# Moving a convolution's channel sums, norm and last step one slot sooner in a hand-ordered two-layer kernel

## The chip, the cores and the metric

The kernel runs on one core of one Trainium2 chip. The core has a matrix engine (TensorE, called PE in the profile), a vector engine (DVE), an activation engine (ACT), a small general engine (POOL) and a queue engine that issues transfers (SP). The metric is the device time of one execution in microseconds (us). Lower is better.

## The reference, cut to what matters

`x` is 256 positions by 2048 channels in float32. A first block (attention branches) gives `x`, and a second block follows. The change lies in the mixing layer of the second block:

```python
y = _rms(h, norm_mix_g)
z = y @ w_in                                   # 2048 -> 4608 columns
za, zb, zc, zd = jnp.split(z, split_at, axis=-1)
oa = _mixer_sgu(za, ...)                       # gated unit
ob = _mixer_shortconv(zb, sc_conv_w)           # 3 taps
oc = _mixer_conformer(zc, cf_conv_w, ...)      # 31 taps, then layer norm, then silu
od = _mixer_pool(zd, pool_w, pool_scale)       # windowed means, then a product
h = h + jnp.concatenate([oa, ob, oc, od], axis=-1) @ w_out

def _mixer_conformer(z, conv_w, conv_b, ln_g, ln_b):
    a, g = jnp.split(z, 2, axis=-1)
    h = a * jax.nn.sigmoid(g)
    h = _causal_dwconv(h, conv_w) + conv_b
    h = _ln(h, ln_g, ln_b)                     # mean and variance over 512 channels
    return jax.nn.silu(h)
```

A feed-forward layer, a gated product with `p` and a last norm follow.

## The kernel before

All large products stream float32 weights from memory. Each weight tile is a "unit": SP loads it into `raw` (5 buffers), ACT copies it into `hi` (4 buffers, rounded to the matrix engine's fast format), DVE writes the rest `raw - hi` into `lo` (in the place of `raw`), and PE makes three products per block, hi x hi, hi x lo and lo x hi (the helper `three`, lines 477 to 479). There are 370 units in one fixed order (`plan`). Groups of four units make one output tile of 512 columns, in one of two halves of PSUM tile `psA`.

Each engine runs its own program, and the order in each is written by hand. For every unit number u, PE runs `side(u)` (small extra products into `psB`) and then `unit(u)`. ACT and DVE run `side(u)`, then `split(u + 3)` (the hi copy on ACT, line 855; the lo subtraction on DVE, line 1244), and after the last unit of a group `post(group)`. For u in `EARLY`, ACT makes its split ahead of its side work. ACT's `split(u + 3)` waits until PE has finished unit u - 1, and DVE's waits for ACT's. So every step is a slot of its engine's queue: a wait in it holds back all that stands behind it. Nothing else ties the slots of the engines together, and DVE may run a slot behind PE.

The units around the change, all of the mixing layer of the second block: 170 to 177 (the convolution's inputs), 178 to 181 `v2`, 182 to 185 `u2`, 186 to 189 `zd`, 190 to 193 `scc`, 194 to 197 `sch`, 198 to 201 `bg`, and 202 to 217 `out2`, the product with `w_out`. Units 178 to 181 and 202 to 217 are of kind N, those of the other names of kind T: 4 blocks x 4 column groups x 3 = 48 matmuls of 256 columns. The four units of one `out2` group take the mixers' parts in `MIX_ORDER` and wait for the semaphore `mix_low` 1, 2, 3, 4.

The side work that matters:

- The 31-tap convolution runs on DVE, channel block by channel block, on `CA`: 124 instructions of line 1443 and 1445 (`conv_tap`), spread over the slots 177 to 194, most with seven. Each adds one to `conv_taps`. The last four stand at the head of DVE's slot 194.
- `channel_sum(psB[:, 0, 0:256], CA, ...)` (line 749) is PE's: four products with a matrix of ones that add up the 512 channels. It waits for `conv_taps` 124, before `unit(u)` of its slot.
- ACT copies the mean to `ST` (line 1045, semaphore `cm_made`). DVE subtracts it (line 1581, `ca_centered`). ACT squares (line 1047, `cv_squared`). PE adds up the squares (line 749 again, `var_dotted`). DVE makes the inverse root (lines 1585 and 1212 to 1217) and scales (line 1587, `ca_normed`). ACT applies gain and bias and makes a tanh (lines 1056, 1058, `cn_tanh`). DVE finishes the silu (line 1607, `cn_made`). ACT and DVE write the hi and lo parts for `out2` (lines 951 and 1460).
- The pooling mixer: `pool_sums` and `pool_means` on DVE (lines 1465 to 1480, semaphore `pool_ready`), its product on PE (line 799, `pool_dotted`), then ACT's and DVE's hi and lo parts (lines 1051 and 1611).
- The short convolution: lines 1590 to 1604 on DVE.
- A helper `finish` makes DVE or ACT wait for the instruction just issued.

Of the kernel before, what the change touches and what calls it, by code (L numbers as in the profile page):

```python
# [10 lines left out]
ACT = mybir.ActivationFunctionType  # L11
# [48 lines left out]

K16 = [[(4 * q + k, 4 * q + k) for k in range(4)] for q in range(4)]
K8 = [[(8 * q + k, 8 * q + k) for k in range(8)] for q in range(2)]
MIX_ORDER = (0, 3, 2, 1)


def plan(A):
# [60 lines left out]
def build_hybrid(nc, A, C, out, scratch):  # L127
    with ExitStack() as ctx:
# [98 lines left out]
        P2 = B[:, 1:3, :].rearrange("p a b -> p (a b)")[:, 0:1088].rearrange("p (c n) -> p c n", c=4)  # L227
        PA = B4[:, :].rearrange("p (c n) -> p c n", c=4)
        SCt = B4[:, 0:1040].rearrange("p (c n) -> p c n", c=4)
        SQ = PW[:, 0:2, :].rearrange("p g d -> p (g d)")  # L230

        psA = ctx.enter_context(nc.psum_tensor("psA", [128, 2, 1024], F32))
        psB = ctx.enter_context(nc.psum_tensor("psB", [128, 2, 1024], F32))
# [106 lines left out]
        TOPK = {21 + n: (2 * n, 2 * n + 1) for n in range(4)}  # L340
        FORGET = {27 + h: h for h in range(4)}
        ATTEND = {s + i: (b, i) for b, s, n in ((0, 32, 6), (1, 43, 6), (2, 59, 11), (3, 75, 6)) for i in range(n)}
        EARLY = (196, 199, 200)
        ATTENDED = {38: 0, 49: 1, 72: 2, 81: 3}
        MERGE = {95 + 20 * f: f for f in range(4)}
        TURN1 = {160 + 4 * f: f for f in range(4)}
# [128 lines left out]
        def tensor_program(e):  # L475
# [276 lines left out]
            def side(u):  # L752
                if u == 1:
                    turn_x(1)
                if u == 6:
                    vectors()
                    e.wait_ge(rd_made, 1)
                    e.wait_ge(xl_made, 3)
                    e.matmul(psB[:, 0, 0:256], ONE, RD[:, :], start=True, stop=True).then_inc(rx_spread, 1)
                if u == 7:  # L760
                    biases()
                if u == 12:
                    spread()
                if u in HEADS:
                    index_heads(HEADS[u][0] // 4)
                if u == 26:
                    forget_sums()
                if u in FORGET:
                    forget_head(FORGET[u])
                if u in ATTEND:  # L770
                    attend(*ATTEND[u])
                if u in ATTENDED:
                    attended(ATTENDED[u])
                if u in MERGE:
                    merge(MERGE[u])
                if u in TURN1:
                    e.wait_ge(h_made, TURN1[u] + 1)
                    turn_h(FIRST + TURN1[u], TURN1[u])
                if u == 172:
                    e.wait_ge(srd_made, 1)  # L780
                    e.wait_ge(ss2_made, 4)
                    e.matmul(psB[:, 0, 0:256], ONE, ST[:, 0, :], start=True, stop=True).then_inc(sb_dotted, 1)
                if u == 175:
                    e.wait_ge(sw_landed, 16)
                    e.wait_ge(sb_made, 1)
                    for h in range(4):
                        x = e.transpose(psB[:, 0, 128 * h:128 * h + 128], B[:, 1, 128 * h:128 * h + 128], ID[:, :])
                    x.then_inc(sw_turned, 1)
                if u == 196:
                    e.wait_ge(conv_taps, 124)  # L790
                    e.wait_ge(sw_made, 1)
                    channel_sum(psB[:, 0, 0:256], CA, cm_dotted)
                if u == 198:
                    ps, w4 = c4(psB[:, 1, :]), c4(B[:, 3, :])
                    e.wait_ge(pool_ready, 1)
                    e.wait_ge(pw_landed, 16)
                    e.wait_ge(sgu_made, 1)
                    for g in range(4):
                        x = e.matmul(ps[:, g, :], PW[:, g, :], w4[:, g, :], start=True, stop=True)
                    x.then_inc(pool_dotted, 1)  # L800
                if u == 198:
                    e.wait_ge(cv_squared, 1)
                    channel_sum(psB[:, 0, 512:768], CB, var_dotted)
                if u in TURN2:
                    e.wait_ge(bank_dve, freed(("out2", TURN2[u])))
                    turn_h(SECOND + TURN2[u], TURN2[u])
                if u == 221:
                    ps = psB[:, 0, 0:512].rearrange("p (k t) -> p k t", k=2)
                    e.wait_ge(p_landed, 16)
                    e.wait_ge(ss3_made, 4)  # L810
                    for k in range(2):
                        for t in range(2):
                            x = e.transpose(ps[:, k, 128 * t:128 * t + 128], PP[:, t, 128 * k:128 * k + 128], ID[:, :])
                    x.then_inc(p_turned, 1)
                if u in TURNH:
                    j = TURNH[u]
                    e.wait_ge(bank_dve, freed(("fu", j)))
                    e.wait_ge(flip_low, HIDDEN + j)
                    flip(lambda t, k: HB[:, t, 128 * k:128 * k + 128], 1)
                if u in TURN3:  # L820
                    e.wait_ge(bank_dve, freed(("down", 8 + TURN3[u])))
                    turn_h(THIRD + TURN3[u], TURN3[u])
# [17 lines left out]
        def scalar_program(e):  # L840
# [112 lines left out]
            def side(u):  # L953
# [86 lines left out]
                if u == 194:  # L1040
                    e.wait_ge(sgu_made, 1)
                    part_high(c4(B[:, 3, :]), 0, 0.5)
                if u == 196:
                    e.wait_ge(cm_dotted, 1)
                    e.activation(ST[:, 0, :], psB[:, 0, 0:256], ACT.Copy, scale=1.0 / 512).then_inc(cm_made, 1)
                    e.wait_ge(ca_centered, 1)
                    e.activation(CB[:, :, :], CA[:, :, :], ACT.Square).then_inc(cv_squared, 1)
                if u == 198:
                    e.wait_ge(pool_dotted, 1)
                    for g in range(4):  # L1050
                        x = e.activation(YH[:, 12 + g, :], c4(psB[:, 1, :])[:, g, :], ACT.Copy, scale=VC[:, 76 + g:77 + g])
                    x.then_inc(mix_high, 1)
                if u == 199:
                    e.wait_ge(ca_normed, 1)
                    for c in range(4):
                        x = e.activation(CA[:, c, :], CA[:, c, :], ACT.Identity, scale=VC[:, 68 + c:69 + c], bias=VC[:, 72 + c:73 + c])
                    finish(x)
                    e.activation(CB[:, :, :], CA[:, :, :], ACT.Tanh, scale=0.5).then_inc(cn_tanh, 1)
                if u == 200:
                    e.wait_ge(cn_made, 1)  # L1060
                    part_high(CA[:, :, :], 2, 0.5)
                if u in TURN2:
                    f = TURN2[u]
                    high(SECOND + f, XH[:, 4 * f:4 * f + 4, :], 1, scale_cols(32, f))
# [136 lines left out]
        def vector_program(e):  # L1201
# [281 lines left out]
            def side(u):  # L1483
# [89 lines left out]
                    gelu_poly(B[:, 3, :], B[:, 2, :], 2)  # L1573
                if u == 194:
                    part_low(c4(B[:, 3, :]), 0, 0.5, 1)
                    pool_sums()
                if u == 195:
                    pool_means()
                if u == 196:
                    e.wait_ge(cm_made, 1)  # L1580
                    e.tensor_tensor(CA[:, :, :], CA[:, :, :], over(ST[:, 0, :], 4), ALU.subtract).then_inc(ca_centered, 1)
                if u == 198:
                    v_, y_, w_ = ST[:, 0, :], ST[:, 1, :], ST[:, 2, :]
                    e.wait_ge(var_dotted, 1)
                    finish(e.tensor_scalar(v_, psB[:, 0, 512:768], 1.0 / 512, EPS, ALU.mult, ALU.add))
                    rsqrt(v_, y_, w_)
                    e.tensor_tensor(CA[:, :, :], CA[:, :, :], over(y_, 4), ALU.mult).then_inc(ca_normed, 1)
                    y = c4(B[:, 2, :])
                    e.wait_ge(sb_made, 1)
                    finish(e.tensor_tensor(SQ, SB[:, :], SB[:, :], ALU.mult))  # L1590
# [2 lines left out]
                    for c in range(4):  # L1593
                        e.tensor_scalar(y[:, c, :], SCt[:, c, 0:256], VC[:, 81 + c:82 + c], None, ALU.mult).then_inc(short_taps, 1)
                if u == 199:
                    y = c4(B[:, 2, :])
                    for j in (1, 2):
                        for c in range(4):
                            e.wait_ge(short_taps, 4 * j - 3 + c)
                            e.scalar_tensor_tensor(out=y[:, c, :], in0=SCt[:, c, j:j + 256],  # L1600
                                                   scalar=VC[:, 81 + 4 * j + c:82 + 4 * j + c], in1=y[:, c, :],
                                                   op0=ALU.mult, op1=ALU.add).then_inc(short_taps, 1)
                    e.wait_ge(short_taps, 12)
                    finish(e.tensor_tensor(y, y, over(SB[:, :], 4), ALU.mult))
                if u == 200:
                    e.wait_ge(cn_tanh, 1)
                    e.scalar_tensor_tensor(out=CA[:, :, :], in0=CB[:, :, :], scalar=1.0, in1=CA[:, :, :], op0=ALU.add,
                                           op1=ALU.mult).then_inc(cn_made, 1)
                    e.wait_ge(mix_high, 2)
                    for g in range(4):  # L1610
                        x = e.scalar_tensor_tensor(out=YL[:, 12 + g, :], in0=c4(psB[:, 1, :])[:, g, :], scalar=VC[:, 76 + g:77 + g],
                                                   in1=YH[:, 12 + g, :].bitcast(F32), op0=ALU.mult, op1=ALU.subtract)
                    x.then_inc(mix_low, 1)
                    part_low(CA[:, :, :], 2, 0.5, 3)
                if u in TURN2:
                    f = TURN2[u]
                    low(SECOND + f, XL[:, 4 * f:4 * f + 4, :], XH[:, 4 * f:4 * f + 4, :], 1, scale_cols(32, f))
# [240 lines left out]
```

## Time and profile before

| | |
|---|---|
| median of 3 runs | 2116.52 us (2116.45 to 2117.03) |
| the profiled execution's own time | 2116.6 us |
| its span in the trace | 2114.8 us |
| PE busy | 2101.7 us, 99% |
| PE weight loads busy (beside the matmuls) | 1788.5 us, 85% |
| DVE busy | 1215.1 us, 57% |
| ACT busy | 901.8 us, 43% |
| bytes moved | 398.34 MB, mean 188 GB/s |

The span is the time from the first to the last instruction of the profiled execution; the time of the execution has 1.8 us more around it. An engine's busy time counts its own instructions, not its waits. A matmul's shown duration overlaps the next one's, since they are pipelined, so the step from start to start is what one costs. For an fp32 product that isn't in the fast format the trace keeps two records for one matmul instruction, so a channel sum of four matmuls has eight. The granted clock is the share of full speed at which TensorE's clock ran.

### The profile page before, as it was taken

What the parts mean: (1) busy time and instruction counts of PE and PEld (TensorE: products, weight loads), DVE (VectorE), ACT (ScalarE), POOL (GpSimd) and SP (SyncE); (2) the same over time, 40 slices, a digit from 0 to 9 for tenths busy, and PEclk for the clock granted to TensorE, in tenths of its full rate; (3) what the DMA queues carried; (4) which work ended last, traced back from release to release, by engine and by line L of the source; (5) the groups of instructions that cost most, each with busy time, mean ns of one, the idle gap of its engine ahead of it and who ended that gap; (6) DMA issues with size and microseconds to landing.
All of it is one profiled execution on the core that took longest, in us unless ns stands there. A gap on an engine that the chain in (4) does not pass through costs nothing.

```text
span 2114.8 us, 24862 instructions
## 1 busy us (share of the span) xinstructions
PE 2101.7 (99%) x10607; PEld 1788.5 (85%) x10607; DVE 1215.1 (57%) x1211; ACT 901.8 (43%) x858; POOL 21.1 (1%) x40
## 2 busy tenths in 40 slices
PE   9999999999999999999999999999999999999998
PEld 8888888888888888888999888888888888888887
DVE  5576555665545544456889855545445454454555
ACT  5444443544443443445354444343333433334443
POOL 2000000000000000000000000000000000000000
PEclk9999999999999999999999999999999999999999
DMA  8655555555655555575655556555555555565553
GB/s 245 212 178 178 166 171 182 171 175 173 199 182 196 192 188 197 192 246 180 206 187 171 179 179 195 189 187 191 198 188 191 184 194 196 187 195 182 195 201 120
DMA packets 224685, 398.34 MB, mean 188 GB/s; under 512 B 11154, under 2 KB 56458, under 8 KB 224320
## 3 DMA queue, kind: packets, MB, share of 16 engines
q1 hardware_dynamic: 221296, 387.64, 56.0%
q0 software_dynamic: 2528, 8.00, 1.3%
q8 instruction: 84, 1.38, 0.3%
q10 hardware_dynamic: 752, 1.12, 0.1%
q14 instruction: 25, 0.20, 0.0%
HBM read 394.62 MB, written 2.12 MB: 188 GB/s over the span
## 4 chain that ended last, share of the span: by engine, by line
PE 95%; DVE 4%; ACT 1%; issue 0%; ACTq 0%
PE psA L477 27%; PE psA L479 27%; PE psA L478 27%; PE psA L530 6%; PE psA L534 3%; DVE CA L1445 1%; PE psB L589 1%; DVE lo L1244 1%; PE psB L689 0%; PE psB L715 0%; PE psA L826 0%; PE psB L637 0%; PE psB L749 0%; ACT hi L855 0%; PE psB L676 0%
## 5 line engine op out<-in xcount | busy, mean ns | idle before, releaser
L1244 DVE TENSOR_TENSOR lo<-raw,hi 128x2048 fp32r<-128x2048 f32 x369 | 837.1, 2272 | 618.2 <-ACT hi L855 616.0
L855 ACT ACTIVATE hi<-raw 128x2048 fp32r<-128x2048 f32 x369 | 699.6, 1900 | 685.4 <-PE psA L479 583.2
L477 PE MATMUL psA<-hi,XHL 128*128 128x512 f32 x1632 | 637.9, 391 | 0.0
L479 PE MATMUL psA<-hi,XHL 128*128 128x512 f32 x1632 | 633.9, 388 | 0.0
L478 PE MATMUL psA<-lo,XHL 128*128 128x512 f32 x1632 | 633.4, 388 | 0.0
L479 PEld LDWEIGHTS psA<-hi,XHL 128*128 128x128 f32 x1632 | 306.3, 188 | 63.6
L477 PEld LDWEIGHTS psA<-hi,XHL 128*128 128x128 f32 x1632 | 306.5, 188 | 62.6 <-issue 0.4
L478 PEld LDWEIGHTS psA<-lo,XHL 128*128 128x128 f32 x1632 | 306.6, 188 | 61.7
L477 PE MATMUL psA<-hi,YH 128*128 128x512 f32 x608 | 237.2, 390 | 0.0
L479 PE MATMUL psA<-hi,YL 128*128 128x512 f32 x608 | 236.6, 389 | 0.0
L478 PE MATMUL psA<-lo,YH 128*128 128x512 f32 x608 | 236.6, 389 | 0.0
L477 PE MATMUL psA<-XHL,hi 128*128 128x256 f32 (+1 forms) x528 | 150.2, 284 | 1.2 <-DVE lo L1284 1.2
L478 PE MATMUL psA<-XHL,hi 128*128 128x256 f32 (+1 forms) x528 | 149.3, 283 | 0.0
L479 PE MATMUL psA<-XHL,lo 128*128 128x256 f32 (+1 forms) x528 | 149.3, 283 | 0.0
L530 PE MATMUL psA<-XHL,hi 128*128 128x512 f32 x576 | 138.6, 393 | 0.0
L479 PEld LDWEIGHTS psA<-hi,YL 128*128 128x128 f32 x608 | 114.1, 188 | 23.7
L477 PEld LDWEIGHTS psA<-hi,YH 128*128 128x128 f32 x608 | 114.1, 188 | 23.5
L478 PEld LDWEIGHTS psA<-lo,YH 128*128 128x128 f32 x608 | 114.2, 188 | 23.4
L530 PEld LDWEIGHTS psA<-XHL,hi 128*128 128x128 f32 x576 | 105.9, 188 | 21.5 <-issue 0.6
L477 PEld LDWEIGHTS psA<-XHL,hi 128*128 128x128 f32 (+1 forms) x528 | 100.7, 191 | 1.7 <-DVE XHL L1291 1.6
L478 PEld LDWEIGHTS psA<-XHL,hi 128*128 128x128 f32 (+1 forms) x528 | 100.7, 191 | 0.2
L479 PEld LDWEIGHTS psA<-XHL,lo 128*128 128x128 f32 (+1 forms) x528 | 100.7, 191 | 0.0
(355 smaller groups left out, 1273.6 us busy)
## 6 DMA issues: line engine op xcount, KB each, us to landing
raw<-in_w_in_dram SPq DMA_DIRECT2D x159, 1024.0 KB, 5.1
raw<-in_w_gate_dram SPq DMA_DIRECT2D x44, 1024.0 KB, 5.2
raw<-in_w_up_dram SPq DMA_DIRECT2D x44, 1024.0 KB, 5.2
raw<-in_w_down_dram SPq DMA_DIRECT2D x44, 1024.0 KB, 5.1
raw<-in_w_out_dram SPq DMA_DIRECT2D x32, 1024.0 KB, 5.1
raw<-in_w_branch_dram SPq DMA_DIRECT2D x16, 1024.0 KB, 5.0
raw<-in_w_ple_gate_dram SPq DMA_DIRECT2D x16, 1024.0 KB, 5.0
raw<-in_w_in_dram SPq DMA_DIRECT2D x16, 512.0 KB, 4.7
```

Of the source, the lines that this page charges most:

```text
L477: e.matmul(dst, A2[0], B2[0], start=first, stop=False, skip_group_check=True)
L478: e.matmul(dst, A2[0], B2[1], start=False, stop=False, skip_group_check=True)
L479: return e.matmul(dst, A2[1], B2[0], start=False, stop=last, skip_group_check=True)
L530: e.matmul(both, hh[:, s], XHL[:, kb, :, :].rearrange("p a t -> p (a t)"), start=i == 0 and n < 2, stop=False, skip_group_check=True)
L534: x = e.matmul(both[:, 256:512], ll[:, s], XH[:, kb, :], start=False, stop=i == len(g.parts) - 1 and n >= 14, skip_group_check=True)
L589: x = e.transpose(ps[:, k, 128 * t:128 * t + 128], src(t, k), ID[:, :])
L855: e.activation(hi[u % H][:, 0:m], raw[u % R][:, 0:m], ACT.Copy).then_inc(hi_made, 1)
L1244: e.tensor_tensor(lo[u % R][:, 0:m], raw[u % R][:, 0:m], hi[u % H][:, 0:m].bitcast(F32), ALU.subtract).then_inc(lo_made, 1)
L1445: x = e.scalar_tensor_tensor(out=CA[:, c, :], in0=HP[:, c, j:j + 256], scalar=CW[:, 4 * j + c:4 * j + c + 1], in1=CA[:, c, :], op0=ALU.mul ...
```

## The change

The convolution's steps after its taps are moved to earlier slots, and the pooling mixer's steps behind them. The parts of `out2` are taken in the order 0, 2, 3, 1 (gated unit, convolution, pooling, short convolution) in place of 0, 3, 2, 1. ACT's `EARLY` slots become 195, 198 and 199. A scratch tile `SQ` lies in `SW` and no more in `PW`, since the pooling product reads `PW` later than before relative to it.

| step | engine | slot before | slot after |
|---|---|---|---|
| channel sum of `CA` | PE | 196 | 195 |
| mean, square | ACT | 196 | 195 |
| subtract the mean | DVE | 196 | 195, behind `pool_sums` |
| `pool_sums` / `pool_means` | DVE | 194 / 195 | 195 / 196 |
| channel sum of the squares | PE | 198 | 197 |
| inverse root and scaling | DVE | 198 | 197 |
| short convolution, start | DVE | 198 | 198 |
| gain, bias, tanh | ACT | 199 | 198 |
| end of the silu, its hi and lo parts | DVE, ACT | 200 | 199 |
| pooling product | PE | 198 | 198 |
| its hi part | ACT | 198 | 199, behind the convolution's |
| its lo part | DVE | 200, ahead of the convolution's | 200 |

```diff
-MIX_ORDER = (0, 3, 2, 1)
+MIX_ORDER = (0, 2, 3, 1)
...
-        SQ = PW[:, 0:2, :].rearrange("p g d -> p (g d)")
+        SQ = SW[:, 0:2, :].rearrange("p g d -> p (g d)")
...
-        EARLY = (196, 199, 200)
+        EARLY = (195, 198, 199)
...
# tensor_program, side(u)
-                if u == 196:
+                if u == 195:
                     e.wait_ge(conv_taps, 124)
                     e.wait_ge(sw_made, 1)
                     channel_sum(psB[:, 0, 0:256], CA, cm_dotted)
...
-                if u == 198:
+                if u == 197:
                     e.wait_ge(cv_squared, 1)
                     channel_sum(psB[:, 0, 512:768], CB, var_dotted)
...
# scalar_program, side(u)
-                if u == 196:
+                if u == 195:
                     e.wait_ge(cm_dotted, 1)
                     e.activation(ST[:, 0, :], psB[:, 0, 0:256], ACT.Copy, scale=1.0 / 512).then_inc(cm_made, 1)
                     e.wait_ge(ca_centered, 1)
                     e.activation(CB[:, :, :], CA[:, :, :], ACT.Square).then_inc(cv_squared, 1)
                 if u == 198:
-                    e.wait_ge(pool_dotted, 1)
-                    for g in range(4):
-                        x = e.activation(YH[:, 12 + g, :], c4(psB[:, 1, :])[:, g, :], ACT.Copy, scale=VC[:, 76 + g:77 + g])
-                    x.then_inc(mix_high, 1)
-                if u == 199:
                     e.wait_ge(ca_normed, 1)
...
-                if u == 200:
+                if u == 199:
                     e.wait_ge(cn_made, 1)
                     part_high(CA[:, :, :], 2, 0.5)
+                    e.wait_ge(pool_dotted, 1)
+                    for g in range(4):
+                        x = e.activation(YH[:, 12 + g, :], c4(psB[:, 1, :])[:, g, :], ACT.Copy, scale=VC[:, 76 + g:77 + g])
+                    x.then_inc(mix_high, 1)
...
# vector_program, side(u)
                 if u == 194:
                     part_low(c4(B[:, 3, :]), 0, 0.5, 1)
+                if u == 195:
                     pool_sums()
-                if u == 195:
-                    pool_means()
-                if u == 196:
                     e.wait_ge(cm_made, 1)
                     e.tensor_tensor(CA[:, :, :], CA[:, :, :], over(ST[:, 0, :], 4), ALU.subtract).then_inc(ca_centered, 1)
-                if u == 198:
+                if u == 196:
+                    pool_means()
+                if u == 197:
                     v_, y_, w_ = ST[:, 0, :], ST[:, 1, :], ST[:, 2, :]
                     e.wait_ge(var_dotted, 1)
...
+                if u == 198:
                     y = c4(B[:, 2, :])
...
                 if u == 199:
+                    e.wait_ge(cn_tanh, 1)
+                    e.scalar_tensor_tensor(out=CA[:, :, :], in0=CB[:, :, :], scalar=1.0, in1=CA[:, :, :], op0=ALU.add,
+                                           op1=ALU.mult).then_inc(cn_made, 1)
                     y = c4(B[:, 2, :])
...
+                    part_low(CA[:, :, :], 2, 0.5, 2)
                     e.wait_ge(short_taps, 12)
                     finish(e.tensor_tensor(y, y, over(SB[:, :], 4), ALU.mult))
                 if u == 200:
-                    e.wait_ge(cn_tanh, 1)
-                    e.scalar_tensor_tensor(out=CA[:, :, :], in0=CB[:, :, :], scalar=1.0, in1=CA[:, :, :], op0=ALU.add,
-                                           op1=ALU.mult).then_inc(cn_made, 1)
-                    e.wait_ge(mix_high, 2)
+                    e.wait_ge(mix_high, 3)
...
-                    part_low(CA[:, :, :], 2, 0.5, 3)
```

## Rows read from the trace of the kernel before

**Rows 1.** The page: busy time by engine, and the chain that ended last.

```profile
PE 2101.7 (99%) x10607; PEld 1788.5 (85%) x10607; DVE 1215.1 (57%) x1211; ACT 901.8 (43%) x858; POOL 21.1 (1%) x40
...
PE 95%; DVE 4%; ACT 1%; issue 0%; ACTq 0%
```

**Rows 2.** All waits of PE: us in total, times, longest.

```profile
PE psA L826 <- DVE QI L1751: 2.0, 1, 2.0
PE psA L477 <- DVE lo L1284: 1.2, 1, 1.2
PE psB L749 <- DVE CA L1445: 0.3, 1, 0.3
```

**Rows 3.** Timeline of PE, 1129 to 1146: start, us, instructions, idle before.

```profile
1129.99 1.95 PE L744 MATMUL psB<-SW,B 128*128 128x128 f32 x16
1131.69 0.36 PE L477 MATMUL psA<-XHL,hi 128*128 128x256 f32 x1
...
1137.41 0.28 PE L479 MATMUL psA<-XHL,lo 128*128 128x256 f32 x1
1137.53 0.28 PE L477 MATMUL psA<-XHL,hi 128*128 128x256 f32 x1
...
1143.17 0.28 PE L479 MATMUL psA<-XHL,lo 128*128 128x256 f32 x1
1143.70 1.99 PE L749 MATMUL psB<-CA,TR 128*128 128x256 f32 x8 [0.25 <-DVE CA L1445]
1145.35 0.47 PE L477 MATMUL psA<-XHL,hi 128*128 128x256 f32 x1
```

**Rows 4.** All waits of DVE from 1100 to 1200.

```profile
DVE lo L1244 <- ACT hi L855: 1.3, 2, 0.7
DVE YL L1460 <- ACT YH L951: 1.1, 1, 1.1
```

**Rows 5.** Timeline of DVE, 1136 to 1185.

```profile
1136.06 2.29 DVE L1244 TENSOR_TENSOR lo<-raw,hi 128x2048 fp32r<-128x2048 f32 x1
...
1141.98 1.67 DVE L1445 SCALAR_TENSOR_TENSOR CA<-HP,CW,CA 128x256 f32<-128x256 f32 x4
1143.56 1.22 DVE L1460 SCALAR_TENSOR_TENSOR YL<-B,YH 128x1024 fp32r<-128x1024 f32 x1
1144.75 0.11 DVE L1465 MEMSET B<- 128x64 f32 x1
...
1147.04 2.29 DVE L1244 TENSOR_TENSOR lo<-raw,hi 128x2048 fp32r<-128x2048 f32 x1
1149.25 0.68 DVE L1473 TENSOR_TENSOR B<-B 128x512 f32<-128x512 f32 x1
...
1152.62 2.29 DVE L1244 TENSOR_TENSOR lo<-raw,hi 128x2048 fp32r<-128x2048 f32 x1
1154.82 1.22 DVE L1581 TENSOR_TENSOR CA<-CA,ST 128x1024 f32<-128x1024 f32 x1
...
1162.32 0.41 DVE L1585 TENSOR_SCALAR ST<-psB 128x256 f32<-128x256 f32 x1
...
1167.57 1.23 DVE L1587 TENSOR_TENSOR CA<-CA,ST 128x1024 f32<-128x1024 f32 x1
1168.71 0.42 DVE L1590 TENSOR_TENSOR PW<-SB 128x256 f32<-128x256 f32 x1
...
1183.15 1.22 DVE L1460 SCALAR_TENSOR_TENSOR YL<-CA,YH 128x1024 fp32r<-128x1024 f32 x1
```

**Rows 6.** Timeline of ACT, 1142 to 1149.

```profile
1143.07 5.50 ACT L855 ACTIVATE hi<-raw 128x2048 fp32r<-128x2048 f32 x3
1148.47 0.36 ACT L1045 ACTIVATE ST<-psB 128x256 f32<-128x256 f32 x1
```

**Rows 7.** Timeline of PE where the execution begins.

```profile
2.02 4.64 PE L826 MATMUL psA<-QI 128*128 128x256 f32 x10 [2.02 <-DVE QI L1751]
6.59 0.28 PE L828 MATMUL psB<-ID,VN 16*128 16x16 f32 x1
```

**Rows 8.** Windows at the end: us, PE, PEld, DVE, ACT, POOL, granted clock, DMA.

```profile
2105.00:2106.00 1.00, 0.20 (x2) 0.00 (x0) 0.20 (x1) 0.77 (x3) 0.00 (x0) 1.00 1.02 379
...
2109.00:2109.50 0.50, 0.00 (x0) 0.00 (x0) 0.43 (x3) 0.14 (x1) 0.00 (x0) 0.96 0.00 0
2109.50:2110.00 0.50, 0.00 (x0) 0.00 (x0) 0.50 (x1) 0.50 (x2) 0.00 (x0) 0.50 0.00 0
```

## The prediction

> **What bounds the kernel.** I read the page first: PE is busy for 99% of the span and makes up 95% of the chain that ended last [rows 1]. Then I asked for every wait of PE. There are three, 3.5 us together, and two of them (2.0 and 1.2 us) lie where the execution begins. The third is the channel sum of line 749, which waits 0.3 us for a convolution tap of line 1445 [rows 2]. So behind the first few us PE has no idle time that this change could take away, except these 0.3 us. And whatever wait the change adds to PE goes to the end in full, since no later idle time of PE is there to absorb it.
>
> The third view is the timeline around that one wait. On PE the product of line 744, which stands behind unit 193, begins at 1129.99. Unit 194 begins at 1131.69. It has 48 matmuls, 0.12 us from start to start (1137.41 to 1137.53), so 5.76 us, which puts the beginning of unit 195 near 1137.5, and its last matmul starts at 1143.17. The channel sum of slot 196 then begins at 1143.70, 0.25 us after PE ran dry, and unit 196 follows at 1145.35 [rows 3]. On DVE the last four taps begin at 1141.98 and take 1.67 us, so they end at about 1143.65 [rows 5]. The tap's end, PE's idle 0.25 us and the start of the channel sum fit one another. The reader is to see that in slot 196 PE meets the taps almost exactly as they end.
>
> **Part 1, the channel sum one slot sooner: where the time goes.** In the changed kernel PE comes to this wait before unit 195, at about 1137.5. The question is when the 124th tap ends there. On DVE no instruction ahead of the last tap is moved: the change of DVE's slots starts behind the lo part of line 1460, which follows the taps. From 1100 to 1200 DVE waited three times only, for 2.4 us in all [rows 4], and none of these waits lies between 1136 and 1144, where one instruction follows the other; the taps are late since DVE is full, not since it waits for PE. ACT's moved steps also stand behind slot 194. So the last tap still ends at about 1143.65, and the channel sum still begins at 1143.70. PE idles from about 1137.65 (the last matmul of unit 194 started at 1137.41 and takes 0.28 us) to 1143.70: 6.0 us in place of 0.25.
>
> What PE loses is one unit: before, unit 195 was done in these 5.76 us, and now it comes behind the channel sum. After the channel sum before stood unit 196 at 1145.35; now unit 195 stands there and unit 196 begins 5.76 us later, at 1151.1. From both sides: if the taps ended 0.25 us sooner for some reason, the loss would be 5.5; if PE needs as long to take up work again as the first matmul of unit 196 shows (0.47 for 0.28 us), 5.95. I take 5.8 us.
>
> **Part 2, the clock behind a stall.** The trace of before has no PE stall of this length in mid-course, so its effect on the clock is bounded by the two ends of the execution. At the end, PE's last matmul lies in the first 0.20 us of the window from 2105, and the granted clock is at 1.00 until the window from 2109.0 to 2109.5, where its mean is 0.96, and then 0.50 [rows 8]: it fell to the lower level (1.2 GHz) some 4.3 us after the last matmul. The stall that I expect is 6.0 us. At the beginning, ten records of 256 columns take from 2.02 to 6.59 [rows 7], 0.46 us each, where eight records of the same shape in the channel sum took 1143.70 to 1145.35, 0.206 each [rows 3]. (The profile's clock column shows 1.00 there; the durations are those of the lower level.) So PE ran for about 4.6 us at the lower level before it came to 2.4 GHz.
>
> Put behind the stall, this would cost: eight records of the channel sum at 0.46 instead of 0.206 us, 3.7 us for 1.65, a loss of 2.0; and the 0.9 us left of 4.6 in unit 195's matmuls, where half speed loses about half, 0.45. Together 2.5 us. Lower bound 0 (the clock holds), upper bound 3.5 (the lower level lasts 2 us longer than at the beginning). I take 2.5, since 6.0 us of idleness is longer than the 4.3 us after which the clock fell at the end.
>
> The Trainium skill ("TensorE: Matmul & The Clock Gate", "HAM oscillation — how this bites in real kernels") says that a pause of the matrix engine in mid-kernel can drop its clock to half, and that it must work for some time before it gets full speed back. By that rule the sum has Part 2 in it and comes to 2124.8; without it, it would be 2122.3. The fall in [rows 8] agrees with the rule; no row here shows one between two stretches of work.
>
> **Part 3, the rest of the moved chain: costs nothing, and gains nothing.** Nothing of it is new work: the instructions and their shapes are the same, no transfer is issued by any of them, and SP and POOL aren't touched. What can cost is a later `split` behind a new wait. I follow the slots with the durations of the rows, from a channel sum that ends at 1145.4 (with the clock's 2 us, 1147.4; PE's own times shift as much or more).
> - DVE slot 194 ends with the lo split, which can begin once ACT's copy, begun at 1143.07 [rows 6], is there at 1145.0: done 1147.2. `pool_sums` takes from 1144.75 to 1147.04 in [rows 5], so 2.3: 1149.5. ACT has by then made its early split and the mean (0.36 us [rows 6]). The mean is subtracted by 1150.7, ACT's square of about 1.1 us is there by 1151.8, and PE wants it before unit 197, at 1156.9: 5 us spare. Behind DVE's wait for the mean stands its split for unit 198, done at 1152.9; PE wants it at about 1166.
> - `pool_means` (1149.25 to 1152.62, 3.4 us [rows 5]) ends at 1156.3, the split for unit 199 at 1158.5. PE wants `pool_ready` before unit 198, at about 1164.5: 8 us spare.
> - Slot 197: the sum of the squares is there at 1158.6. From line 1585 to the end of line 1587 took 1162.32 to 1168.8, 6.5 us [rows 5]: 1165.2, and behind it the split for unit 200, done at 1167.4. PE wants that at about 1177.6: 10 us spare.
> - Slots 198 to 200 hold the same DVE work as before in another order (1168.71 to 1184.4 with splits in it [rows 5]). It ends at about 1184, and the third unit of `out2` wants the pooling part at about 1200. PE has 6 us to spare at the tightest, the split for unit 202.
>
> So the convolution's part is ready a few us sooner relative to PE, but its reader never waited: [rows 2] have no wait for `mix_low`. If this slack weren't there, each late split would cost PE its lateness; the smallest slack is 5 us.
>
> **The sum.** Against the profiled execution's own time of 2116.6 us (span 2114.8): + 5.8 + 2.5 = 2124.9. The runs' median is 0.1 us lower, so the time for the runs is 2124.8 us.
>
> **The rivals.**
> - The clock holds through the stall. Then only the unit's time is lost: 2116.5 + 5.8 = 2122.3. For it: the granted clock at the end held for 4.3 us, so the stall outlasts it by less than 2 us, and where the fall comes may vary. Against it: 6.0 is still the longer time.
> - Another stall behind the first one: DVE's slots 195 to 197 now put lo splits behind waits for ACT and PE. It would show as line 477 waiting for line 1244. It decides if a link of the chain slips by over the 5 us of slack. Price: what it slips beyond that, some 2 us, so about 2127. Against it: every slack above is twice an instruction's length or more.
> - On the other side, faster or no change: DVE reaches its last tap sooner, before PE runs dry. For this the work of 1136.06 to 1141.98 on DVE (a split, line 1456, the `scc` step) would have to be gone from before the taps. It decides from a last tap that ends by about 1137.7, 6 us sooner; then even the 0.25 us of idle time go, and the time is 2116.3. I see nothing in the diff that moves any of it, and the wait is for all 124 taps, not for the first channel block's.
> - The change doesn't do what it says: the compiled order would be the written one, as the queues are in order, so I give it nothing of its own; it is in the case before.
>
> **Chances.** Stall and clock, 2124.8: 0.62. Clock holds, 2122.3: 0.23. A further stall, 2127: 0.07. No added stall of weight: 0.08, of which 0.02 for faster. The range holds the first two: from 2121.8 (5.5 for the unit, less 0.2 for the runs' spread) to 2126.0 (5.95 and 3.5). The likeliest case alone spans 2123.5 to 2126.0. A measurement of this kernel tells about 0.2% (4.2 us) from no change, so slower begins at 2120.7: the first three cases are all beyond it. Slower 0.92, same 0.06, faster 0.02.
>
> **What would show each step.** Right: PE's waits have line 749 on line 1445 with about 6 us in place of 0.3; the last taps still begin near 1142.0 and the channel sum at 1143.7; the windows around 1141 to 1148 show a granted clock below 1.00, and the eight records of the channel sum take about 3.7 us; no other wait of PE is longer than before. Wrong: the channel sum starts sooner than 1143, or PE waits for a lo split later, or the channel sum after the stall takes 1.65 us, which would be the clock that holds.

## The result, and the profile after

The changed kernel takes 2124.64 us in the median of 6 runs (2124.14 to 2125.13), the kernel before 2116.78 (2116.4 to 2117.28, 6 runs on the same chip). The ratio is 1.0037 (95% interval 1.0027 to 1.0048), so the change makes the kernel slower by 7.9 us. The profiled execution took 2125.03 us, with a span of 2123.2 against 2114.8 before.

All waits of PE in the changed kernel, to be read against [rows 2] (columns: us in total, times, longest):

```profile
PE psB L749 <- DVE CA L1444: 6.0, 1, 6.0
PE psA L826 <- DVE QI L1751: 2.0, 1, 2.0
PE psA L477 <- DVE lo L1283: 1.2, 1, 1.2
```

The two waits at the beginning are as before. The channel sum's wait for the last tap (line 1444 here, 1445 before) has grown from 0.3 to 6.0 us, and no wait for a lo split or for `mix_low` has come up. PE's timeline there, to be read against [rows 3]:

```profile
1137.18 0.28 PE L479 MATMUL psA<-XHL,lo 128*128 128x256 f32 x1
1143.46 3.78 PE L749 MATMUL psB<-CA,TR 128*128 128x256 f32 x8 [6.00 <-DVE CA L1444]
1146.68 0.78 PE L477 MATMUL psA<-XHL,hi 128*128 128x256 f32 x1
1147.25 0.41 PE L478 MATMUL psA<-XHL,hi 128*128 128x256 f32 x1
1147.47 0.41 PE L479 MATMUL psA<-XHL,lo 128*128 128x256 f32 x1
...
1149.60 0.30 PE L477 MATMUL psA<-XHL,hi 128*128 128x256 f32 x1
1149.74 0.28 PE L478 MATMUL psA<-XHL,hi 128*128 128x256 f32 x1
1149.86 0.28 PE L479 MATMUL psA<-XHL,lo 128*128 128x256 f32 x1
...
1191.94 0.40 PE L477 MATMUL psA<-hi,YH 128*128 128x512 f32 x1
```

The channel sum starts at 1143.46, where it started at 1143.70 before; this execution began its weight stream 0.23 us sooner. The unit that follows is 195, not 196. The eight records of the sum now reach from 1143.46 to 1146.68, 3.2 us in place of 1.65, and the unit's first matmuls are 0.21 us apart, where from 1149.74 they are 0.12 us apart as everywhere else. The windows around the pause show why (columns: window, its length, PE, PEld, DVE, ACT and POOL busy with counts, granted clock, DMA share, GB/s):

```profile
1138.00:1139.00 1.00, 0.00 (x0) 0.00 (x0) 1.00 (x2) 0.00 (x0) 0.00 (x0) 1.00 0.52 82
1139.00:1140.00 1.00, 0.00 (x0) 0.00 (x0) 0.97 (x3) 0.00 (x0) 0.00 (x0) 0.70 0.76 176
1140.00:1141.00 1.00, 0.00 (x0) 0.00 (x0) 0.96 (x2) 0.00 (x0) 0.00 (x0) 0.50 1.01 383
...
1148.00:1149.00 1.00, 1.00 (x7) 1.00 (x7) 0.96 (x2) 0.00 (x0) 0.00 (x0) 0.50 0.00 0
1149.00:1150.00 1.00, 1.00 (x8) 1.00 (x8) 0.97 (x2) 0.00 (x0) 0.00 (x0) 0.68 0.00 0
1150.00:1151.00 1.00, 1.00 (x11) 1.00 (x10) 1.00 (x2) 0.46 (x1) 0.00 (x0) 1.00 0.00 0
```

A mean of 0.70 in the window from 1139 is a fall to 0.50 at about 1139.4, some 2 us after PE ran dry. The mean of 0.68 in the window from 1149 is a rise at about 1149.6, and it fits the step from 0.21 to 0.12 us in the timeline. So PE worked for 6.2 us at the lower level (1.2 GHz).

The first matmul of `out2` (operand `YH`) starts at 1191.94. Before, it started at 1183.53, as this row shows:

```profile
1183.53 0.40 PE L477 MATMUL psA<-hi,YH 128*128 128x512 f32 x1
```

That is 8.4 us later, and the spans differ by 8.4 us too. Everything that the change costs lies ahead of `out2`, and nothing of it is given back behind.

On DVE the last taps stand where they stood in [rows 5], within the 0.25 us by which this execution is ahead, and the moved steps follow:

```profile
1141.73 1.67 DVE L1444 SCALAR_TENSOR_TENSOR CA<-HP,CW,CA 128x256 f32<-128x256 f32 x4
...
1144.74 2.29 DVE L1243 TENSOR_TENSOR lo<-raw,hi 128x2048 fp32r<-128x2048 f32 x1 [0.20 <-ACT hi L855]
...
1149.29 1.22 DVE L1578 TENSOR_TENSOR CA<-CA,ST 128x1024 f32<-128x1024 f32 x1
...
1161.63 0.42 DVE L1584 TENSOR_SCALAR ST<-psB 128x256 f32<-128x256 f32 x1 [3.19 <-PE psB L749]
...
1180.65 1.21 DVE L1459 SCALAR_TENSOR_TENSOR YL<-CA,YH 128x1024 fp32r<-128x1024 f32 x1
```

DVE now waits 3.2 us for the sum of the squares (line 1584), and PE doesn't feel it. The convolution's lo part (line 1459) starts at 1180.65 in place of 1183.15 [rows 5], and 11 us ahead of `out2` in place of 0.4. The change does what it was written to do; its reader had no use for it.

### The profile page after: what moved, and what is told of

Its sections match the earlier page's. It is cut to its first block, busy times and chain, and to the rows that moved or that the text cites. A ratio compares the mean times of both kernels' runs of the same rounds, so it can differ in the third digit from the quotient of the medians.

```text
span 2123.2 us, 24862 instructions
## 1 busy us (share of the span) xinstructions
PE 2104.4 (99%) x10607; PEld 1791.1 (84%) x10607; DVE 1215.5 (57%) x1211; ACT 902.4 (43%) x858; POOL 21.2 (1%) x40
## 4 chain that ended last, share of the span: by engine, by line
PE 95%; DVE 4%; ACT 1%; issue 0%; ACTq 0%
PE psA L477 27%; PE psA L479 27%; PE psA L478 27%; PE psA L530 6%; PE psA L534 3%; DVE CA L1444 1%; PE psB L589 1%; DVE lo L1243 1%; PE psB L749 0%; PE psB L689 0%; PE psB L715 0%; PE psA L826 0%; PE psB L637 0%; ACT hi L855 0%; PE psB L677 0%
```

## The experiments

Theory: PE's earlier wait for the last tap is the whole cost. It costs one unit's time (5.76 us), and the pause lowers the clock, which costs some 2 us more. Rivals: the moved chain costs by itself, or the part above 5.76 us is something else than the clock.

### The first channel sum back in its slot

```diff
-                if u == 195:
+                if u == 196:
                     e.wait_ge(conv_taps, 124)
```

> The changed kernel with one edit: PE's first channel sum stands in slot 196 again, all other steps stay in their new slots. My theory (the whole cost is PE's wait for the last tap in slot 195, with the clock's fall behind it): PE reaches the sum as the taps end, about 0.25 us of wait as before. The second sum in slot 197 now follows one unit behind the first, while DVE's subtraction and ACT's square need about 6 us from it, so a second wait of 0 to 1 us may show. 2116.6 to 2117.6 us, no stretch below full clock. Rival (the moved chain on DVE and ACT costs by itself, by lo splits behind new waits): 2118 to 2124 us, with PE waiting at line 477 for a lo split.

Measured: 2117.23 us (2117.09 to 2117.69), before on the same chip 2116.72; ratio 1.0002 (0.9993 to 1.0011). Its PE waits:

```profile
PE psB L749 <- ACT CB L1047: 0.5, 1, 0.5
PE psB L749 <- DVE CA L1444: 0.2, 1, 0.2
```

One line of the change put back takes away 7.4 of the 7.9 us. What is left, 0.5 us, goes with the second wait, 0.5 us for ACT's square, since here the second sum follows one unit behind the first; it was expected at 0 to 1 us. The other moved steps cost nothing that shows beside it.

### The first channel sum sooner, and nothing else

```diff
# the kernel before
-                if u == 196:
+                if u == 195:
                     e.wait_ge(conv_taps, 124)
```

> The kernel before with one edit: PE's first channel sum stands in slot 195 in place of 196; nothing else is moved. My theory: the same stall of 6.0 us, one unit's time lost and a fall of the clock, so 2124 to 2125 us, all of the change's cost from this one edit. Rival (the cost is shared with the other moves): less than 2123 us.

Measured: 2124.17 us (2123.78 to 2124.68), ratio 1.0035 (1.0022 to 1.0047). This edit alone brings 7.45 of the change's 7.9 us. The profile shows the same wait and a shorter time at the lower clock:

```profile
PE psB L749 <- DVE CA L1445: 6.0, 1, 6.0
```

```profile
1143.64 3.48 PE L749 MATMUL psB<-CA,TR 128*128 128x256 f32 x8 [6.01 <-DVE CA L1445]
```

Its granted clock fell at about 1139.9 and was back at about 1146.7, 3.0 us after PE took up work; in the changed kernel it was 6.2 us. To compare executions that began their weight stream at different times, I count from the start of the first channel sum to the start of `out2`: 39.83 us before (1143.70 to 1183.53), 48.48 in the changed kernel (1143.46 to 1191.94), and 47.07 here (1143.64 to 1190.71). That is 7.24 us more than before: the unit's 5.76 and 1.5 for the clock. So behind the same pause the clock's part was 1.5 us in this profile and 2.9 in that of the changed kernel.

### The pause filled with work

The edit adds products that nobody reads. They write the place in `psB` that the channel sum overwrites, and their number is the only thing that differs between the five kernels of this kind:

```diff
# the changed kernel
                 if u == 195:
-                    e.wait_ge(conv_taps, 124)
                     e.wait_ge(sw_made, 1)
+                    for _ in range(14):
+                        e.matmul(psB[:, 0, 0:256], ONE, TR[:, :], start=True, stop=True)
+                    e.wait_ge(conv_taps, 124)
                     channel_sum(psB[:, 0, 0:256], CA, cm_dotted)
```

> The changed kernel with 14 extra fp32 products of 256 columns (28 records, about 5.8 us at full clock) in slot 195 of PE ahead of the wait for the taps; they write the place that the channel sum overwrites and nobody reads them. They stand in the time in which PE sat idle, so the channel sum begins as before them. My theory (5.8 us of the cost are the unit that comes later, the rest is work at the lower clock): the granted clock stays at full, the eight records of the channel sum take 1.65 us, and the time is 2122.3 to 2122.8 us, about 2.2 us under the changed kernel. Rival (the part above 5.8 us is not the clock but PE starting up or other moves): no gain, 2124.6 us. Rival (idleness is what costs, so filling it gives it all back): 2117 us.

Measured: 2122.5 us (2122.25 to 2122.98), ratio 1.0027 (1.0016 to 1.0038).

```profile
1138.00 6.21 PE L792 MATMUL psB<-TR 128*128 128x256 f32 x28
1144.16 1.99 PE L749 MATMUL psB<-CA,TR 128*128 128x256 f32 x8
1145.80 0.47 PE L477 MATMUL psA<-XHL,hi 128*128 128x256 f32 x1
```

PE has no pause, the granted clock is 1.00 in every window from 1136 to 1152, the eight records of the sum take 1.64 us again (1144.16 to 1145.80), and the kernel does more work and is 2.1 us faster than the changed one. What stays is 5.8 us above before, the one unit that comes later. That separates the two parts of the cost. The first rival (the rest isn't the clock) wanted no gain and the second (filling gives all back) 2117 us; neither came.

### The pause filled in part

How long may a pause be before it costs the clock? The same edit with fewer products.

With 3 products:

> The same with 3 extra products (6 records, about 1.2 us), which leaves PE idle for about 4.8 us, longer than the 4.3 us at the end of the execution before. Theory: the clock falls in all or nearly all executions, 2123.8 to 2124.8 us. Rival (a fall needs the whole 6 us): 2122.5 us.

Measured: 2124.68 us (2124.55 to 2126.01), ratio 1.0038 (1.0024 to 1.0053).

With 7:

> The changed kernel with 7 extra fp32 products (14 records, about 2.9 us at full clock, read by nobody) ahead of the wait of slot 195, so PE's idle time shrinks from 6.0 to about 3.1 us while the channel sum begins as before. It asks how long a pause PE can have before its clock falls. In the changed kernel's profile the clock fell 2.2 us after PE ran dry, at the end of the execution before it took 4.3 us. Theory (the pause is what counts, with a fall somewhere from 2.2 to 4.3 us): some executions fall, some don't, 2122.3 to 2124.6 us, the median near 2123.4. Rival (3.1 us are short enough): 2122.5 us as with the whole pause filled. Rival (any long wait costs the whole 2.2 us): 2124.6 us.

Measured: 2125.53 us (2125.34 to 2126.33), ratio 1.0042 (1.0027 to 1.0057).

With 9:

> The changed kernel with 9 extra fp32 products (18 records, about 3.7 us, read by nobody) ahead of the wait of slot 195, which leaves PE idle for about 2.2 us. With 7 products, 3.0 us idle, the granted clock fell as the pause ended. Theory (a pause of 2.2 us, as long as the shortest after which a profile showed a fall, is the edge): the clock holds in most executions, 2122.3 to 2123.0 us. Rival (any pause of PE in mid-course lowers the clock): 2124 us or more.

Measured: 2123.23 us (2123.07 to 2123.85), ratio 1.0031 (1.0019 to 1.0043).

With 11:

> The same with 11 extra products (22 records, about 4.5 us), which leaves PE idle for about 1.4 us. Theory: the clock holds in every execution, 2122.3 to 2122.8 us, as with the pause filled. Rival (any pause lowers the clock): 2124 us or more.

Measured: 2123.43 us (2123.14 to 2123.73), ratio 1.0032 (1.0021 to 1.0044).

The timelines, in the order 3, 7, 9, 11 products:

```profile
1143.55 3.78 PE L749 MATMUL psB<-CA,TR 128*128 128x256 f32 x8 [4.73 <-DVE CA L1446]
```

```profile
1143.87 3.67 PE L749 MATMUL psB<-CA,TR 128*128 128x256 f32 x8 [2.98 <-DVE CA L1446]
```

```profile
1143.86 1.99 PE L749 MATMUL psB<-CA,TR 128*128 128x256 f32 x8 [2.10 <-DVE CA L1446]
```

```profile
1143.73 1.99 PE L749 MATMUL psB<-CA,TR 128*128 128x256 f32 x8 [1.24 <-DVE CA L1446]
```

The second number is the sum's extent: 3.78 and 3.67 us behind pauses of 4.7 and 3.0 us, 1.99 behind 2.1 and 1.2 us, as in [rows 3]. The clock fell in the first two profiles and held in the last two. One execution of each kernel was profiled; whether the clock held in the others isn't shown. In the profile with 3.0 us it fell just as the pause ended, as its windows show (columns as above):

```profile
1142.00:1143.00 1.00, 0.00 (x0) 0.00 (x0) 1.00 (x4) 0.73 (x1) 0.00 (x0) 1.00 0.34 131
1143.00:1144.00 1.00, 0.13 (x1) 0.13 (x1) 1.00 (x4) 1.00 (x2) 0.00 (x0) 0.94 0.00 0
1144.00:1145.00 1.00, 1.00 (x3) 0.82 (x4) 0.95 (x1) 1.00 (x1) 0.00 (x0) 0.50 0.00 0
```

These profiles can be taken apart at the start of `out2` (all in us; the last column is the span less that start):

| extra products | pause | first sum to `out2` | more than before | `out2` to the end |
|---|---|---|---|---|
| 0 (the changed kernel) | 6.0 | 48.48 | 8.65 | 931.3 |
| 3 | 4.7 | 48.48 | 8.65 | 931.3 |
| 7 | 3.0 | 47.25 | 7.42 | 932.6 |
| 9 | 2.1 | 45.58 | 5.75 | 932.5 |
| 11 | 1.2 | 45.58 | 5.75 | 932.0 |
| 14 | none | 45.58 | 5.75 | 931.3 |

Where the clock held, the cost ahead of `out2` is the one unit, 5.75 us, and nothing else. Where it fell, it cost a further 2.9, 2.9 and 1.7 us.

Three of the medians still missed what I expected. The kernel with 7 products is the slowest of all, where I expected the median between the two levels, and those with 9 and 11 lie 0.7 and 0.9 us above the one with 14, where I expected at most 2123.0 and 2122.8 us. The last column shows where this comes from: behind `out2` these three profiles take 0.7 to 1.3 us more than the others and than before (931.3). It is the issue of the first two stores from ACT's queue. Changed kernel, 7, 9 and 11 products:

```profile
2110.89 0.96 ACTq L1197 DMA_DIRECT2D out_dram<-PJ  x2
```

```profile
2110.05 2.25 ACTq L1199 DMA_DIRECT2D out_dram<-PJ  x2
```

```profile
2108.47 2.10 ACTq L1199 DMA_DIRECT2D out_dram<-PJ  x2
```

```profile
2108.22 1.74 ACTq L1199 DMA_DIRECT2D out_dram<-PJ  x2
```

These stores stand in ACT's queue ahead of the last tanh steps, so 0.8 to 1.3 us more there go straight to the end. With 14 products and with 3 the profiled executions had 0.96 again. With that taken off, the profiled execution with 7 products would be at about 2124.2 us (2125.5 less 1.3), between the two levels though nearer the upper one, and those with 9 and 11 at about 2122.6 and 2122.4 (2123.73 less 1.14, 2123.14 less 0.78). Why the issue takes longer in some of these programs, no run here shows.

### The taps one slot sooner, on both kernels

Here the cause is taken away: eight taps per slot instead of seven, so that the last four end ahead of a lo split and the `scc` step.

```diff
-CHUNK = 7
+CHUNK = 8
```

On the changed kernel:

> The changed kernel with eight convolution taps per slot of DVE in place of seven (CHUNK = 8), so the last four taps stand in slot 193, ahead of a lo split (2.2 us), line 1455 (1.2 us) and the three instructions of the scc step (2.5 us). The same instructions, another place. My theory (the stall is the end of the last tap, and nothing else of the change costs): the last tap ends about 5.9 us sooner, near 1137.6, PE waits 0 to 0.5 us, the clock stays at full, and the time is 2116.3 to 2117.0 us. Rival (the earlier chain costs by itself): over 2118 us. Rival (heavier slots make lo splits late): PE waits at line 477 for line 1243, 2117.5 to 2120 us.

Measured: 2116.6 us (2116.32 to 2117.18), ratio 0.9999 (0.999 to 1.0009).

```profile
1134.33 1.66 DVE L1444 SCALAR_TENSOR_TENSOR CA<-HP,CW,CA 128x256 f32<-128x256 f32 x4
```

```profile
1138.19 1.89 PE L749 MATMUL psB<-CA,TR 128*128 128x256 f32 x8
1151.76 1.99 PE L749 MATMUL psB<-CB,TR 128*128 128x256 f32 x8 [0.18 <-ACT CB L1047]
```

The taps end at 1136.0, 7.4 us sooner than in the changed kernel (I expected 5.9; the four last taps of the convolution's first half have also gone ahead of a split, and DVE began the second half 1.5 us sooner). PE finds them done in slot 195, doesn't wait, and the 7.9 us are gone with every step of the change in its new slot. The second sum, though, now waits for ACT's square, 0.18 us by its row. DVE and ACT came to it no sooner than in the changed kernel, where DVE's subtraction began at 1149.29:

```profile
1149.39 1.23 DVE L1578 TENSOR_TENSOR CA<-CA,ST 128x1024 f32<-128x1024 f32 x1
```

```profile
1150.65 1.06 ACT L1047 ACTIVATE CB<-CA 128x1024 f32<-128x1024 f32 x1 [3.77 <-DVE CA L1578]
```

The subtraction stands behind a lo split and `pool_sums` in DVE's queue, so the sooner sum doesn't bring it forward.

On the kernel before:

> The kernel before with eight convolution taps per slot in place of seven and nothing else. It is the control for the same edit on the changed kernel. Theory: the last tap ends 6 us or more ahead of PE's slot 196, the idle 0.25 us of the channel sum goes, and the time is 2116.3 to 2116.7 us, no different from before within the measurement. Rival (heavier slots of DVE make lo splits late): 2118 us or more, and then the changed kernel with that edit would have gained from the change.

Measured: 2115.95 us (2115.82 to 2116.19, 10 runs), before on the same chip 2116.68 (2116.37 to 2117.22, 14 runs); ratio 0.9996 (0.9987 to 1.0006). The channel sum has no wait any more:

```profile
1143.13 1.89 PE L749 MATMUL psB<-CA,TR 128*128 128x256 f32 x8
```

The ranges of the two don't overlap, but the interval of the ratio holds 1, so this is at most a gain of 0.7 us. It lies below the 2116.3 to 2116.7 that I expected, since I counted the wait as its 0.25 us. From the start of unit 195's last matmul to that of the sum it is 0.53 us before (1143.17 to 1143.70) and 0.12 here (1143.01 to 1143.13), and the sum's own eight records take 1.54 us in place of 1.65: the short wait cost 0.5 us in all.

It is the fastest kernel of this study, and the one to hold against the changed kernel with the same edit, which is 0.65 us slower (2116.6; their ranges don't overlap either, though the intervals of some 2 us to each side don't resolve it). In the profiles, `out2` begins here 39.73 us behind the first sum's start:

```profile
1182.86 0.40 PE L477 MATMUL psA<-hi,YH 128*128 128x512 f32 x1
```

With both edits it begins 45.92 us behind it:

```profile
1184.11 0.40 PE L477 MATMUL psA<-hi,YH 128*128 128x512 f32 x1
```

Of these 5.76 us are the one unit more that lies between. The rest, 40.16 us, is 0.4 more than 39.73, which fits the second sum's wait for ACT's square. So with its input there the changed order costs almost nothing, but it gains nothing either and, by these two profiles, loses 0.4 us against its control.

## Why the prediction was right

The forecast was 2124.8 us in a range of 2121.8 to 2126.0; measured are 2124.64. By its steps:

- **Part 1, the unit.** Right in place and size. The last tap did not move, PE waits 6.0 us as forecast, and the filled pause shows what is left when the clock holds: 2122.5 less 2116.7 is 5.8 us, the 5.76 us of 48 matmuls. Both single edits of the first sum (back in its slot 0.5 us, alone in slot 195 7.45 us over before) show that it is this step and no other.
- **Part 2, the clock.** Right in kind, and its size was found from the wrong two numbers that made up for each other. I took 2.5 us. In the profiled execution it is 8.65 - 5.76 = 2.9 us (from the sum's start to `out2`: 48.48 us after, 39.83 before). The records of the sum cost 0.40 us each at the lower level and not the 0.46 of the execution's beginning, so the sum lost 1.6 and not 2.0; but the lower level lasted 6.2 us behind the pause and not 4.6, so unit 195 worked for 3.0 us at it and lost 1.3 (0.21 in place of 0.12 us from matmul to matmul) and not 0.45. That the sum of the two came within 0.4 us is luck. The medians, 7.9 less 5.8, give 2.1 us as the usual loss. The bounds of 0 and 3.5 us held all of it.
- **The fall itself.** I argued that 6.0 us is longer than the 4.3 us of the execution's end [rows 8]. The conclusion held, but one fall was too little to argue from. In the changed kernel the clock fell 2 us after PE ran dry, so 4.3 us was no threshold; over the falls in mid-course and at the ends of all eleven profiles the delay goes from 1.9 to 5.0 us. A stall of 6.0 us is longer than all of them. It fell in each of the four profiles with pauses from 3.0 to 6.0 us. (The 2.2 us that two expectations above name as the shortest delay are those of the kernel with the single edit; in the changed kernel it was 1.9.)
- **Part 3, the slack.** Right. PE had no new wait behind the sum. DVE's 3.2 us of waiting for the second sum, which I hadn't drawn, follow PE's loss by the clock: it is 0.4 us in the three profiles in which the clock held, 2.1 with 7 products and 3.2 where the clock cost 2.9. The 5 us that PE had to spare before the second sum rest on PE being one unit late. With the taps one slot sooner PE isn't late, and the slack is gone: the second sum waits.
- **The rivals.** "The clock holds" was worked out as 2122.3, and the kernel with the filled pause, which is this case made on purpose, is at 2122.5. "DVE reaches its last tap sooner" was put at 2116.3 with the point from which it decides at a tap end of 1137.7; with the taps ending at 1136.0 the kernel is at 2116.6. "A further stall", as a wait for a lo split, appeared nowhere here; PE waited for the chain only at the second sum, 0.5 us where it was brought within one unit of the first and 0.2 us where PE no longer stalled.
- **The Trainium skill's rule** on pauses ("TensorE: Matmul & The Clock Gate", "HAM oscillation — how this bites in real kernels") agrees with the trace: the granted clock is at 0.50 from about 1139.4 to 1149.6. With the pause filled by useless products it stayed at 1.00, and 2.1 us came back.

## What to carry to other kernels

On the engine that is busy all the time, ask of every step that is moved sooner whether its input is there at the new place: here the wait row of 0.3 us and the end of its releaser said that there was no room at all, and one slot cost one whole unit. A result that is ready sooner is worth nothing unless some wait row names its reader. A pause of the matrix engine can cost more than its own length: here the stall cost one unit, 5.76 us, and the slow work behind it a further 1.5 to 2.9 us. Take away what makes the engine wait, or, if it must wait, give it the work that comes next before the wait, as the kernel with the first sum back in its slot does. And hold a fix against its own control: only the kernel before with the same eight taps per slot showed that the new order itself loses a little.

## What the runs showed of the hardware

- The granted clock fell 1.9, 2.2, 3.0 and 4.1 us after PE ran dry in mid-course (changed kernel, first sum alone, 7 and 3 products), and 2.0 to 5.0 us after the last matmul at the ends of the eleven profiles (4.3 in the kernel before, 5.0 in the changed kernel with the taps sooner). Pauses of 6.0, 4.7 and 3.0 us brought a fall, pauses of 2.1 and 1.2 us none in their profiles. Since some delays were as short as 1.9 us, one profile with a pause of 2.1 us and no fall doesn't show that such a pause is safe.
- Behind the same pause of 6.0 us the lower level lasted 6.2 us of work in one profile (the changed kernel) and 3.0 us in another (first sum alone); behind 4.7 and 3.0 us it lasted 6.2 and 3.4 us.
- A wait of the channel sum that its row gives as 0.25 us cost PE 0.5 us, counted from matmul to matmul, against the kernel in which it doesn't wait.
- An fp32 product of 256 columns has two records of 0.206 us at 2.4 GHz; at 1.2 GHz behind the pause they took 0.40 us each, at the execution's beginning, where the clock column shows 1.00, 0.46.
- The issue of the first two stores from ACT's queue took 0.96 or 0.97 us in eight profiles and 1.74 to 2.25 us in three of the kernels with extra products; that of the last two took 0.95 us in those three as well. The reason stays open.
